# TensorE products whose results nobody reads, in stages that have no work for it

## The chip, the cores and the metric

The kernel runs on one core of one Trainium2 chip. The metric is device time in microseconds (us), lower is better. TensorE is the matrix engine (PE in the profile, its weight loads PEld), VectorE is DVE, ScalarE is ACT, GpSimd is POOL and SyncE (SP) issues the loads. TensorE's clock is granted at one of two levels, 1.2 and 2.4 GHz; the profile writes the granted clock as a share of 2.4 GHz.

## The reference, cut to what matters

Two transformer layers on one sequence of 512 tokens with 1024 features, all in float32. Everything that is computed matters here only as a row of stages: products (TensorE), and between them norms and selections (the other engines).

```python
# layer 1
h = rms_norm(x, ln1_g);  proj = h @ w_in
aq, ak = rms_norm(q, q_norm_g), rms_norm(k, k_norm_g)          # per head of 64
attn = rms_norm(neighbourhood_attention(aq, ak, av, rpb), attn_out_g)
dn   = rms_norm(gated_delta_both_directions(...), out_norm_g) * silu(z)   # q, k l2-normed per head of 128
x = x + concat([attn, dn]) @ w_out
h = rms_norm(x, ln2_g)
#   64 experts in 8 groups: best group, best two experts in it, for each of 512 tokens
y[token] += gate * (silu(h @ w_gate[e]) * (h @ w_up[e])) @ w_down[e]
# layer 2
h = rmsnorm(x);  proj = h @ w_in2
merged = sigmoid(g_ml)*(mlstm(...) @ w_ml) + sigmoid(g_sc)*(short_conv(...) @ w_sc) + sigmoid(g_sb)*(stick_breaking(...) @ w_sb)
x = x + merged @ w_out2
x = x + square(relu(rmsnorm(x) @ w_up2)) @ w_down2
return rmsnorm(x)
```

## The kernel before

The program is a list of 54 stages. Each engine runs its part of stage k, drains its pipeline, adds one to its own counter and waits until the three others (of TensorE, ScalarE, VectorE and GpSimd) have done the same (`close`, L2402 and L2405). So a stage is as long as its longest engine, and an engine that has no part in a stage stands at that barrier. `together()` joins several parts into one stage. SyncE doesn't take part in the barrier and loads weights ahead of it, into four buffers.

Big products (`dense`, `mlp`, `experts`) read 1 MB units of weights, which ScalarE and VectorE split into a high and a low float32r part (`whi`, `wlo`); TensorE makes three products of each pair (high*high, high*low, low*high), 512 columns each, into PSUM banks (L325, L342, L1575, L1589, L2308, L2323). Small things, such as transposes (`transposes`, L396), gram matrices and the delta rule, go in plain float32; of such a product the trace has two records at 128x512, one where it is a transpose.

The stages that the change touches:

- `normalise`: ScalarE squares, VectorE sums and scales. TensorE has no part. It comes nine times before `transposes` of what was normalised (`n1`, `nq`+`nk`, `nao`, `ndq`+`ndk`, `ndo`, `n2`, `h2an`, `ny`+`h2bn`, `h3n`).
- `transposes`: TensorE transposes four 128x128 tiles into each of up to eight banks; ScalarE takes each bank (L406) and, where the result is split, VectorE takes it again (L414).
- `gate_z` and `split_into` (`smix`) around the transposes of the delta rule's result, and then the dense stage `wout`.
- `beta_exp`, a short stage ahead of `delta`. In `delta`, `pe_gram` (L949) makes two products for the first batch; VectorE and ScalarE make `lo_m` and `pw` from them, on which `pe_step` (L967, L969) waits.
- `route` ends on VectorE, `select` builds the one-hot matrices `sel` on VectorE and GpSimd, `sort_tokens` multiplies with them (L1433).
- `combine` gathers the experts' rows by DMA and adds them to `x` on VectorE; it and the norm `h2an` follow each other, then come transposes and a small product (`small_product`, L673).
- `stick`: TensorE makes the scores of heads 0 and 1 (L2152, operands of 64 partitions, and the mask L2157), then `sums(0)` (L2169) waits for ScalarE's and VectorE's softplus of head 0.

Of the kernel before, what the change touches and what calls it, by code (L numbers as in the profile page):

```python
# [33 lines left out]
TT = T // P  # L34
D = 1024
# [48 lines left out]
def build(nc, x_in, cols_in, rows_in, consts_in, bias_in, w_in, w_ab, w_out, w_router, w_gate, w_up, w_down,  # L84
# [186 lines left out]

    def dense(tag, sources, mode, out_fn, by, acc_hi=act_hi, acc_lo=act_lo, loaded=0, lent=None, act_also=None, dve_also=None, pool_part=None):
# [224 lines left out]
    normalise("n1", x[:, :, :], xn[:, :, :], stat_a[:, 0:TT], stat_b[:, 0:TT], D, sq_b[:, :])  # L497
# [19 lines left out]
    with together():  # L517
        normalise("nq", heads64(q_tok), heads64(q_tok), stat_q[:, 0, :], stat_q[:, 1, :], DA, sq_a[:, 0, :], extra=DA ** -0.5)
        normalise("nk", heads64(k_tok), heads64(k_tok), stat_q[:, 2, :], stat_q[:, 3, :], DA, sq_a[:, 1, :])
# [119 lines left out]
    with together():  # L639
        load_small("ab", w_ab, ab_w)  # L640
        normalise("nao", o_tok[:, :, :], attn_n[:, :, :], stat_q[:, 0, 0:TT], stat_q[:, 1, 0:TT], 512, sq_o[:, :])
# [164 lines left out]
    with together():  # L806
        normalise("ndq", heads128(dq_tok), heads128(dq_tok), stat_d[:, 0, :], stat_d[:, 1, :], DD, sq_d[:, :], eps_scale=1.0, extra=DD ** -0.5)
        normalise("ndk", heads128(dk_tok), heads128(dk_tok), stat_d[:, 2, :], stat_d[:, 3, :], DD, sq_e[:, :], eps_scale=1.0)
# [79 lines left out]
    beta_exp()  # L888

    def delta():  # L890
# [109 lines left out]
        def pe_part(pe):  # L1000
            pe_gram(pe, batches[0])
            for a in batches:
                old = batches[a.b - 1] if a.b else None
                new = batches[a.b + 1] if a.b + 1 < NB else None
                for s in range(n_steps):
                    for hb in range(2):
                        pe_step(pe, a, s, hb)
                        if old and s == 0 and hb == 1:
                            pe_scan_out(pe, old, 0)
                        if old and 1 <= s <= 3:  # L1010
                            (pe_scan_out if hb else pe_scan_pv)(pe, old, s)
                    if new and s == 5:
                        pe_gram(pe, new)
            pe_scan_out(pe, batches[-1], 0)
            for n in range(1, TT):
                pe_scan_pv(pe, batches[-1], n)
                pe_scan_out(pe, batches[-1], n)
# [191 lines left out]
    normalise("ndo", heads128(dn_o), heads128(dn_n), stat_d[:, 0, :], stat_d[:, 1, :], DD, dn_sq[:, :])  # L1209
# [11 lines left out]
    gate_z()  # L1221
# [16 lines left out]
    split_into("smix", mix, act_hi, act_lo)  # L1238
# [11 lines left out]
    normalise("n2", x[:, :, :], xn2[:, :, :], stat_m[:, 0, :], stat_m[:, 1, :], D, sq_m[:, :])  # L1250
# [166 lines left out]
    select()  # L1417
# [378 lines left out]
    combine()  # L1796
# [10 lines left out]
    def hidden(tag, gain, also=lambda: None):  # L1807

        with together():
            also()  # L1810
            normalise(tag + "n", x[:, :, :], xn3[:, :, :], stat3[:, 0, :], stat3[:, 1, :], D, sq3[:, :])
        transposes(tag + "t", lambda tt, c: xn3[:, tt, c * P:(c + 1) * P], lambda c: col(gain, c))
# [220 lines left out]
    with together():  # L2033
        normalise("ny", yh, yh, stat_y[:, 0, :], stat_y[:, 1, :], DM, sq_y[:, :])
        normalise("h2bn", x[:, :, :], xn3[:, :, :], stat3[:, 0, :], stat3[:, 1, :], D, sq3[:, :])
# [101 lines left out]
    def stick():  # L2137
# [7 lines left out]
        def pe_part(pe):  # L2145
# [37 lines left out]
            scores(1)  # L2183
            for h in range(HS):
                sums(h)
                if h:
                    values(h - 1)
                if h + 2 < HS:
                    scores(h + 2)
# [325 lines left out]
```

## Time and profile before

| | |
|---|---|
| runs of the kernel before | 2804.57, 2872.67, 2864.63 us; median 2864.63 |
| profiled execution, its own time | 2804.5 us |
| its span, first to last instruction | 2802.7 us |
| mean granted TensorE clock in it | 0.938 |
| TensorE busy / weight loads busy | 88% / 75% |
| VectorE / ScalarE / GpSimd busy | 51% / 41% / 12% |
| chain that ended last: TensorE's share | 81% |

The runs lie 68 us apart, and the profiled execution stands beside the shortest of them. All times of the trace below are of that execution, counted from the span's start.

### The profile page before, as it was taken

The page shows a single profiled execution, that of the slowest core. Times are in us where ns is not written, and L with a number is a line of the kernel's source. Part 1 is how long each engine was busy: PE and PEld are TensorE (multiplying, and loading weights), DVE is VectorE, ACT ScalarE, POOL GpSimd, SP SyncE. Part 2 cuts the span into 40 slices and gives each one's busy share as a digit, 9 for nine tenths or more (in the row PEclk, how much of TensorE's full clock was granted, in tenths as well). Part 3 has the DMA queues.
Part 4 walks back from the last instruction along what each step waited for, and adds up shares of the span by engine and source line. Part 5 has one row for each costly group of instructions (what it writes and reads, how often), then busy time and mean ns, then how long its engine had stood idle before and what let it go on. Part 6 is the DMA issues. An engine that isn't in the chain of part 4 may idle for free.

```text
span 2802.7 us, 34731 instructions
## 1 busy us (share of the span) xinstructions
PE 2458.5 (88%) x13304; PEld 2111.1 (75%) x13304; DVE 1434.1 (51%) x1602; ACT 1139.5 (41%) x1350; POOL 339.2 (12%) x178
## 2 busy tenths in 40 slices
PE   5789789863999999997599659999999998899997
PEld 4567679852899999997488448888887887688885
DVE  2344656636399999997321462253222444434333
ACT  2453455321477777775222232212223651222221
POOL 0000010001245445552100000000000000000000
PEclk9899889985999999999799789999999989899998
DMA  5101000020399999998233002223322001132320
GB/s 211 61 2 61 1 1 1 15 95 16 124 377 378 380 380 379 382 382 306 106 97 98 30 1 90 90 90 106 100 95 90 1 1 60 60 106 92 103 90 38
DMA packets 144427, 356.93 MB, mean 127 GB/s; under 512 B 6496, under 2 KB 82400, under 8 KB 127808
## 3 DMA queue, kind: packets, MB, share of 16 engines
q1 hardware_dynamic: 142736, 346.63, 34.8%
q0 software_dynamic: 1584, 8.78, 0.8%
q8 instruction: 78, 1.28, 0.2%
q14 instruction: 29, 0.24, 0.0%
HBM read 336.52 MB, written 18.87 MB: 127 GB/s over the span
## 4 chain that ended last, share of the span: by engine, by line
PE 81%; DVE 9%; ACT 4%; DMA 2%; issue 2%; DVEq 1%; ACTq 1%; POOL 0%; SPq 0%; POOLq 0%; PEldq 0%
PE PS L325 23%; PE PS L342 11%; PE PS L1589 10%; PE PS L2308 6%; PE PS L2323 6%; PE PS L1575 6%; PE PS L969 4%; PE PS L2169 2%; PE PS L396 2%; PE PS L2152 1%; PE PS L2179 1%; PE PS L1433 1%; DVE wlo L249 1%; PE PS L546 1%; PE PS L563 1%
## 5 line engine op out<-in xcount | busy, mean ns | idle before, releaser
L249 DVE TENSOR_TENSOR wlo<-raw,whi 128x2048 fp32r<-128x2048 f32 x246 | 601.6, 2446 | 654.1 <-ACT whi L242 654.1
L242 ACT ACTIVATE whi<-raw 128x2048 fp32r<-128x2048 f32 x246 | 470.4, 1913 | 535.6 <-PE PS L325 180.0
L325 PE MATMUL PS<-act_hi,whi 128*128 128x512 f32 x736 | 286.6, 389 | 3.1 <-DVEq L2402 3.1
L325 PE MATMUL PS<-act_hi,wlo 128*128 128x512 f32 x736 | 286.4, 389 | 0.0
L325 PE MATMUL PS<-act_lo,whi 128*128 128x512 f32 x736 | 286.3, 389 | 0.0
L1553 POOL TENSOR_TENSOR st_lo<-sorted_h,st_hi 128x512 fp32r<-128x512 f32 x64 | 189.6, 2962 | 11.6 <-POOL st_hi L1550 11.6
L342 PE MATMUL PS<-whi,act_hi 128*128 128x512 f32 x448 | 176.6, 394 | 15.8 <-DVEq L2402 15.8
L342 PE MATMUL PS<-wlo,act_hi 128*128 128x512 f32 x448 | 176.1, 393 | 0.0
L342 PE MATMUL PS<-whi,act_lo 128*128 128x512 f32 x448 | 175.9, 393 | 0.0
L249 DVE TENSOR_TENSOR wlo_x<-raw,whi_x 128x2048 fp32r<-128x2048 f32 x64 | 145.7, 2276 | 36.1 <-ACT whi_x L242 36.1
L325 PEld LDWEIGHTS PS<-act_hi,whi 128*128 128x128 f32 x736 | 138.2, 188 | 32.0 <-issue 3.4
L325 PEld LDWEIGHTS PS<-act_hi,wlo 128*128 128x128 f32 x736 | 138.2, 188 | 28.8
L325 PEld LDWEIGHTS PS<-act_lo,whi 128*128 128x128 f32 x736 | 138.2, 188 | 28.5
L1589 PE MATMUL PS<-whi,st_hi 128*128 128x256 f32 x520 | 153.1, 295 | 7.0 <-POOL st_lo L1553 6.9
L1589 PE MATMUL PS<-wlo,st_hi 128*128 128x256 f32 x520 | 147.8, 284 | 0.0
L1589 PE MATMUL PS<-whi,st_lo 128*128 128x256 f32 x520 | 147.4, 284 | 0.0
L1589 PE MATMUL PS<-whi_x,st_lo 128*128 128x256 f32 x504 | 142.7, 283 | 0.0
L1589 PE MATMUL PS<-wlo_x,st_hi 128*128 128x256 f32 x504 | 142.6, 283 | 0.0
L1589 PE MATMUL PS<-whi_x,st_hi 128*128 128x256 f32 x504 | 142.3, 282 | 0.0
L2382 POOL DMA_DIRECT2D gfin<-in_gfin x1 | 0.5, 546 | 1115.3 <-DVEq L2402 1115.3
L1550 POOL CAST st_hi<-sorted_h 128x512 fp32r x64 | 98.0, 1532 | 263.8 <-PE PS L1589 165.9
L242 ACT ACTIVATE whi_x<-raw 128x2048 fp32r<-128x2048 f32 x64 | 122.2, 1910 | 0.7 <-issue 0.3
(507 smaller groups left out, 5233.2 us busy)
## 6 DMA issues: line engine op xcount, KB each, us to landing
raw<-in_w_up SPq DMA_DIRECT2D x80, 1024.0 KB, 5.4
raw<-in_w_down SPq DMA_DIRECT2D x80, 1024.0 KB, 5.2
raw<-in_w_in SPq DMA_DIRECT2D x66, 1024.0 KB, 5.2
raw<-in_w_gate SPq DMA_DIRECT2D x64, 1024.0 KB, 5.9
y_sorted<-y_sb SPq DMA_DIRECT2D x64, 256.0 KB, 4.7
raw<-in_w_out SPq DMA_DIRECT2D x8, 1024.0 KB, 5.2
raw<-in_w_ml SPq DMA_DIRECT2D x4, 1024.0 KB, 5.2
raw<-in_w_sc SPq DMA_DIRECT2D x4, 1024.0 KB, 5.4
```

Of the source, the lines that this page charges most:

```text
L242: nc.scalar.activation(parts(u, wide)[0], raw[:, raw_slot(u), :], ACT.Copy).then_inc(hi_ready, 1)
L249: nc.vector.tensor_tensor(lo, raw[:, raw_slot(u), :], hi.bitcast(F32), ALU.subtract).then_inc(lo_ready, 1)
L325: last = nc.tensor.matmul(ps[:, m, :], a, b, start=(c == 0 and k == 0), stop=(c == KT - 1 and k == 2))
L342: last = nc.tensor.matmul(psum_of(j, i)[:, m, :], a, b, start=(f == 0 and k == 0), stop=(f == KT - 1 and k == 2))
L396: last = nc.tensor.transpose(PS[:, bank + c % 8, tt * P:(tt + 1) * P], src_tile(tt, c), ident)
L969: last = nc.tensor.matmul(o, lhsT[:, hb, tt, :], rhs[:, hb, tt, :], start=True, stop=True)
L1550: nc.gpsimd.tensor_copy(st_hi[:, b, :, 0:blk], src).then_inc(s_cp, 1)
L1553: nc.gpsimd.tensor_tensor(st_lo[:, b, :, 0:blk], src, st_hi[:, b, :, 0:blk].bitcast(F32), ALU.subtract).then_inc(s_stat, 1)
L1575: i = nc.tensor.matmul(PS[:, 3 + 2 * b + half, :], x_[:, b, j, :], w_[:, j, c], start=(j == 0 and k == 0), stop=(j == 1 and k == 2))
L1589: i = nc.tensor.matmul(PS[:, b, k * DE:(k + 1) * DE], x_[:, b, c, :], w_[:, c, :], start=(c == 0 and m == 0), stop=(c == KT - 1 and m == 2))
L2308: i = nc.tensor.matmul(PS[:, 2 * j + m, :], a_, b_, start=(k == 0 and n == 0), stop=(k == KT - 1 and n == 2))
L2323: i = nc.tensor.matmul(PS[:, 4 * p + m, :], a_, b_, start=(y == 0 and n == 0), stop=(y == KT - 1 and n == 2))
```

## The change

A helper `throwaway(n)` gives TensorE n plain float32 products: stationary `ident` (128x128), moving the first four constant matrices side by side (128x512), into PSUM bank 7, each one with start and stop set. They wait for nothing but the stage's start and signal nothing. Thirteen calls join a stage in which TensorE had no part (`hidden` is called twice, so there are fourteen such stages), and two stand in the middle of TensorE's part: 8 products in bank 5 after the first `pe_gram` of `delta`, and 6 after the scores of heads 0 and 1 in `stick`. The last norm, `nf`, gets none. In all 142 products are added: 5, 12, 6, 12, 2, 8, 6, 5, 6, 6, 13, 26, 6, 17, 6 (stick) and 6 (`h3n`). Nothing else is changed.

```diff
--- before.py
+++ after.py
@@ -269,6 +269,14 @@
         stages.append({e: one_after_another([m[e] for m in members if e in m])
                        for e in ("sp", "pe", "act", "dve", "pool") if any(e in m for m in members)})
 
+    def throwaway(n, bank=7):
+
+
+        def pe_part(pe):
+            for _ in range(n):
+                nc.tensor.matmul(PS[:, bank, :], ident, consts[:, 0:4, :].rearrange("p a b -> p (a b)"), start=True, stop=True)
+        return pe_part
+
     def dense(tag, sources, mode, out_fn, by, acc_hi=act_hi, acc_lo=act_lo, loaded=0, lent=None, act_also=None, dve_also=None, pool_part=None):
 
 
@@ -494,7 +502,9 @@
             split_lo(dve, u, u)
 
     add_stage(sp=first_sp, act=first_act, dve=first_dve, pe=lambda pe: pe.wait_ge(s_load, 7 * 16), pool=first_pool)
-    normalise("n1", x[:, :, :], xn[:, :, :], stat_a[:, 0:TT], stat_b[:, 0:TT], D, sq_b[:, :])
+    with together():
+        add_stage(pe=throwaway(5))
+        normalise("n1", x[:, :, :], xn[:, :, :], stat_a[:, 0:TT], stat_b[:, 0:TT], D, sq_b[:, :])
     transposes("t1", lambda tt, c: xn[:, tt, c * P:(c + 1) * P], lambda c: col("ln1", c))
 
 
@@ -515,6 +525,7 @@
     def heads64(t):
         return t[:, :, :].rearrange("p t (h e) -> p (t h) e", e=DA)
     with together():
+        add_stage(pe=throwaway(12))
         normalise("nq", heads64(q_tok), heads64(q_tok), stat_q[:, 0, :], stat_q[:, 1, :], DA, sq_a[:, 0, :], extra=DA ** -0.5)
         normalise("nk", heads64(k_tok), heads64(k_tok), stat_q[:, 2, :], stat_q[:, 3, :], DA, sq_a[:, 1, :])
     with together():
@@ -638,6 +649,7 @@
         add_stage(pool=lambda pool, st: pool.dma_start(w_f32[:, :, :], w_dram).then_inc(s_small, 16))
     with together():
         load_small("ab", w_ab, ab_w)
+        add_stage(pe=throwaway(6))
         normalise("nao", o_tok[:, :, :], attn_n[:, :, :], stat_q[:, 0, 0:TT], stat_q[:, 1, 0:TT], 512, sq_o[:, :])
     transposes("tao", lambda tt, c: attn_n[:, tt, c * P:(c + 1) * P], lambda c: col("attn_out", c), n_c=4, dst_f32=mix)
 
@@ -804,6 +816,7 @@
     sq_d = at("sq_d", o_w + 8 * KB, [P, TT * 512])
     sq_e = at("sq_e", o_w + 16 * KB, [P, TT * 512])
     with together():
+        add_stage(pe=throwaway(12))
         normalise("ndq", heads128(dq_tok), heads128(dq_tok), stat_d[:, 0, :], stat_d[:, 1, :], DD, sq_d[:, :], eps_scale=1.0, extra=DD ** -0.5)
         normalise("ndk", heads128(dk_tok), heads128(dk_tok), stat_d[:, 2, :], stat_d[:, 3, :], DD, sq_e[:, :], eps_scale=1.0)
     dqT = at("dqT", o_b, [P, HD, T])
@@ -885,7 +898,9 @@
             dve.wait_ge(s_e, 1)
             nc.vector.tensor_tensor(bexp[:, :, :], t_a[:, :, :], beta[:, :, :], ALU.mult)
         add_stage(act=act_part, dve=dve_part)
-    beta_exp()
+    with together():
+        add_stage(pe=throwaway(2))
+        beta_exp()
 
     def delta():
 
@@ -999,6 +1014,7 @@
 
         def pe_part(pe):
             pe_gram(pe, batches[0])
+            throwaway(8, 5)(pe)
             for a in batches:
                 old = batches[a.b - 1] if a.b else None
                 new = batches[a.b + 1] if a.b + 1 < NB else None
@@ -1206,7 +1222,9 @@
     dn_sq = at("dn_sq", o_b, [P, TT * 512])
     dn_z = at("dn_z", o_b + 8 * KB, [P, TT, 512])
     dn_n = at("dn_n", o_b + 16 * KB, [P, TT, 512])
-    normalise("ndo", heads128(dn_o), heads128(dn_n), stat_d[:, 0, :], stat_d[:, 1, :], DD, dn_sq[:, :])
+    with together():
+        add_stage(pe=throwaway(6))
+        normalise("ndo", heads128(dn_o), heads128(dn_n), stat_d[:, 0, :], stat_d[:, 1, :], DD, dn_sq[:, :])
 
     def gate_z():
         s_z = local("gz")
@@ -1218,7 +1236,9 @@
             dve.wait_ge(s_z, 1)
             nc.vector.tensor_tensor(dn_n[:, :, :], dn_n[:, :, :], dn_z[:, :, :], ALU.mult)
         add_stage(act=act_part, dve=dve_part)
-    gate_z()
+    with together():
+        add_stage(pe=throwaway(5))
+        gate_z()
     mix_d = mix[:, 4:8, :]
     transposes("tdn", lambda tt, c: dn_n[:, tt, c * P:(c + 1) * P], lambda c: col("dn_out"), n_c=4, dst_f32=mix_d)
 
@@ -1235,7 +1255,9 @@
                 dve.wait_ge(s_h, c // 2 + 1)
                 nc.vector.tensor_tensor(lo[:, c:c + 2, :], src[:, c:c + 2, :], hi[:, c:c + 2, :].bitcast(F32), ALU.subtract)
         add_stage(act=act_part, dve=dve_part)
-    split_into("smix", mix, act_hi, act_lo)
+    with together():
+        add_stage(pe=throwaway(6))
+        split_into("smix", mix, act_hi, act_lo)
 
     def residual_out(eng, st, j, ps, ms):
         s = slice((j // 2) * 512, (j // 2 + 1) * 512)
@@ -1247,7 +1269,9 @@
     sq_m = at("sq_m", o_b, [P, TT * D])
     o_r = o_w + 36 * KB
     stat_m = at("stat_m", o_r, [P, 2, TT])
-    normalise("n2", x[:, :, :], xn2[:, :, :], stat_m[:, 0, :], stat_m[:, 1, :], D, sq_m[:, :])
+    with together():
+        add_stage(pe=throwaway(6))
+        normalise("n2", x[:, :, :], xn2[:, :, :], stat_m[:, 0, :], stat_m[:, 1, :], D, sq_m[:, :])
     NR = NG + NE
     r_w = at("r_w", o_b, [P, KT, NR])
     r_wh = at("r_wh", o_b + 3 * KB, [P, KT, NR], F32R)
@@ -1414,7 +1438,9 @@
             for tt in range(TT - 1):
                 nc.gpsimd.tensor_scalar(sel_t[:, tt, :], iota[:, :], dest[:, 0, tt:tt + 1], None, ALU.is_equal).then_inc(s_first, 1)
         add_stage(act=act_part, dve=dve_part, pool=pool_part)
-    select()
+    with together():
+        add_stage(pe=throwaway(13))
+        select()
 
     def sort_tokens():
 
@@ -1793,7 +1819,9 @@
                     st.then(nc.vector.scalar_tensor_tensor(x[:, tt, :], y_rows[:, k, tt, :], gates[:, k, tt:tt + 1], x[:, tt, :],
                                                            ALU.mult, ALU.add))
         add_stage(sp=sp_part, pool=pool_part, dve=dve_part)
-    combine()
+    with together():
+        add_stage(pe=throwaway(26))
+        combine()
 
 
 
@@ -1808,6 +1836,7 @@
 
         with together():
             also()
+            add_stage(pe=throwaway(6))
             normalise(tag + "n", x[:, :, :], xn3[:, :, :], stat3[:, 0, :], stat3[:, 1, :], D, sq3[:, :])
         transposes(tag + "t", lambda tt, c: xn3[:, tt, c * P:(c + 1) * P], lambda c: col(gain, c))
 
@@ -2031,6 +2060,7 @@
     sq_y = at("sq_y", o_b, [P, TT * D])
     yh = y_tok[:, :, :].rearrange("p t (h e) -> p (t h) e", e=DM)
     with together():
+        add_stage(pe=throwaway(17))
         normalise("ny", yh, yh, stat_y[:, 0, :], stat_y[:, 1, :], DM, sq_y[:, :])
         normalise("h2bn", x[:, :, :], xn3[:, :, :], stat3[:, 0, :], stat3[:, 1, :], D, sq3[:, :])
     transposes("ty", lambda tt, c: y_tok[:, tt, c * P:(c + 1) * P], lambda c: col("ml", c), dst_hi=y_hi, dst_lo=y_lo)
@@ -2181,6 +2211,7 @@
                 last.then_inc(s_av, 1)
             scores(0)
             scores(1)
+            throwaway(6)(pe)
             for h in range(HS):
                 sums(h)
                 if h:
```

Three places of TensorE's order. Between `route` (products with `both`) and `sort_tokens` (products with `sel`), before:

```order
L1381 MATMUL PS<-both,consts 128x64
L1383 MATMUL PS<-both,consts 128x64 x4
L1433 MATMUL PS<-sel,tok_hi 128x512
L1433 MATMUL PS<-sel,tok_lo 128x512
L1433 MATMUL PS<-sel,tok_hi 128x512
L1433 MATMUL PS<-sel,tok_lo 128x512
```

and with the change:

```order
L1405 MATMUL PS<-both,consts 128x64
L1407 MATMUL PS<-both,consts 128x64 x4
L277 MATMUL PS<-consts 128x512 x13
L1459 MATMUL PS<-sel,tok_hi 128x512
L1459 MATMUL PS<-sel,tok_lo 128x512
L1459 MATMUL PS<-sel,tok_hi 128x512
L1459 MATMUL PS<-sel,tok_lo 128x512
```

The thirteen products stand in the stage `select`, between the two; the products around them are the same, at new line numbers.

At the start of `delta`, after the last products of `grams` (with `g`), TensorE's order before:

```order
L834 MATMUL PS<-g,consts 128x4
L835 MATMUL PS<-g,consts 128x4
L949 MATMUL PS<-qeT_129,consts 128x512 x2
L967 MATMUL PS<-consts,pw_119 128x128 x8
L969 MATMUL PS<-pw_119,pwT 128x128 x4
L969 MATMUL PS<-pwT,pw_119 128x128 x4
```

and with the change:

```order
L847 MATMUL PS<-g,consts 128x4
L848 MATMUL PS<-g,consts 128x4
L277 MATMUL PS<-consts 128x512 x2
L964 MATMUL PS<-qeT_129,consts 128x512 x2
L277 MATMUL PS<-consts 128x512 x8
L982 MATMUL PS<-consts,pw_119 128x128 x8
L984 MATMUL PS<-pw_119,pwT 128x128 x4
L984 MATMUL PS<-pwT,pw_119 128x128 x4
```

Two products stand ahead of the gram products (with `qeT`), in the stage `beta_exp`, and eight between those and the transposes of `pw`.

At the start of `stick`, the scores of head 1 (`bqT`, `bkT`, mask) and then the sums of head 0 (`sb_hi`, `sb_lo`), on TensorE before:

```order
L2152 MATMUL PS<-bqT,bkT 128x384
L2152 MATMUL PS<-bqT,bkT 128x256
L2152 MATMUL PS<-bqT,bkT 128x128
L2157 MATMUL PS<-sb_mask,sb_id 128x128 x4
L2169 MATMUL PS<-sb_hi_237,sb_tri 128x512
L2169 MATMUL PS<-sb_lo_234,sb_tri 128x512
L2169 MATMUL PS<-sb_hi_237,sb_one 128x384
```

and with the change:

```order
L2182 MATMUL PS<-bqT,bkT 128x384
L2182 MATMUL PS<-bqT,bkT 128x256
L2182 MATMUL PS<-bqT,bkT 128x128
L2187 MATMUL PS<-sb_mask,sb_id 128x128 x4
L277 MATMUL PS<-consts 128x512 x6
L2199 MATMUL PS<-sb_hi_237,sb_tri 128x512
L2199 MATMUL PS<-sb_lo_234,sb_tri 128x512
L2199 MATMUL PS<-sb_hi_237,sb_one 128x384
```

Six products stand between head 1's mask and head 0's sums.

## Rows read from the trace of the kernel before

**Rows 1.** The page's first two parts: TensorE's busy time, granted clock in slices.

```profile
PE 2458.5 (88%) x13304; PEld 2111.1 (75%) x13304; DVE 1434.1 (51%) x1602; ACT 1139.5 (41%) x1350; POOL 339.2 (12%) x178
...
PEclk9899889985999999999799789999999989899998
```

**Rows 2.** Windows of stages without TensorE: length, busy PE, PEld, DVE, ACT, POOL, PEclk.

```profile
108.10:120.40 12.30, 0.00 (x0) 0.00 (x0) 10.67 (x15) 4.72 (x10) 0.00 (x0) 0.50 0.26 85
203.60:210.00 6.40, 0.00 (x0) 0.00 (x0) 5.11 (x7) 3.68 (x6) 0.55 (x1) 0.74 0.04 10
...
352.00:353.90 1.90, 0.00 (x0) 0.00 (x0) 0.19 (x1) 1.51 (x2) 0.00 (x0) 0.88 0.00 0
...
572.70:578.70 6.00, 0.00 (x0) 0.00 (x0) 4.63 (x4) 3.90 (x4) 0.00 (x0) 0.72 0.00 0
628.50:635.30 6.80, 0.00 (x0) 0.00 (x0) 5.47 (x10) 3.68 (x6) 0.00 (x0) 0.50 0.44 154
684.60:698.30 13.70, 0.00 (x0) 0.00 (x0) 12.28 (x9) 3.90 (x4) 10.34 (x3) 0.50 0.00 0
1326.80:1353.10 26.30, 0.00 (x0) 0.00 (x0) 10.28 (x8) 0.00 (x0) 7.65 (x8) 0.50 0.78 280
...
1641.80:1658.70 16.90, 0.00 (x0) 0.00 (x0) 14.83 (x17) 7.68 (x11) 0.00 (x0) 0.56 0.00 0
...
sum 134.90, PE 0.00 PEld 0.00 DVE 97.78 ACT 52.90 POOL 19.13; mean PE 0.00 PEld 0.00 DVE 6.98 ACT 3.78 POOL 1.37
```

**Rows 3.** Timeline of TensorE in delta, batches 0 and 1: start, length.

```profile
355.43 3.75 PE L949 MATMUL PS<-qeT,consts 128*128 128x512 f32 x4 [3.71 <-ACT qeT L1048]
363.95 0.47 PE L967 MATMUL PS<-consts,pw 128*128 128x128 f32 x1 [4.77 <-DVE lo_m L1131]
...
387.62 1.88 PE L949 MATMUL PS<-qeT,consts 128*128 128x512 f32 x4
389.34 0.83 PE L969 MATMUL PS<-pw,pwT 128*128 128x128 f32 x6
```

**Rows 4.** Windows where TensorE had work, same columns as Rows 2.

```profile
336.20:339.80 3.60, 3.47 (x17) 3.50 (x18) 0.00 (x0) 1.79 (x3) 0.00 (x0) 0.50 0.00 0
353.40:370.50 17.10, 10.03 (x31) 6.61 (x32) 9.93 (x30) 10.05 (x32) 7.18 (x4) 0.50 0.00 0
578.70:582.10 3.40, 3.35 (x8) 2.70 (x9) 0.00 (x0) 0.00 (x0) 0.00 (x0) 0.50 0.00 0
698.30:701.60 3.30, 3.25 (x8) 2.68 (x9) 0.00 (x0) 0.00 (x0) 0.52 (x1) 0.50 0.00 0
1363.80:1367.20 3.40, 1.71 (x16) 1.47 (x14) 3.30 (x6) 2.86 (x5) 0.00 (x0) 1.00 0.00 0
2159.10:2176.20 17.10, 16.03 (x42) 11.07 (x43) 6.83 (x10) 9.76 (x17) 0.00 (x0) 0.50 0.20 62
```

**Rows 5.** Timeline of TensorE around two transposing stages; idle before in brackets.

```profile
27.37 6.23 PE L396 MATMUL PS<-consts,xn 128*128 128x128 f32 x32 [27.37 <-DVEq L2402]
35.68 0.48 PE L342 MATMUL PS<-whi,act_hi 128*128 128x512 f32 x1 [2.08 <-DVEq L2402]
...
36.39 0.63 PE L342 MATMUL PS<-whi,act_lo 128*128 128x512 f32 x1
...
1359.98 5.54 PE L396 MATMUL PS<-consts,xn 128*128 128x128 f32 x32 [35.80 <-DVEq L2402]
1368.64 0.40 PE L673 MATMUL PS<-act_hi,g2h 128*8 128x512 f32 x1 [3.13 <-DVE g2l L663]
```

**Rows 6.** Groups by line: VectorE's and ScalarE's reading of transposed banks.

```profile
L414 DVE SCALAR_TENSOR_TENSOR act_lo<-PS,cols,act_hi 128x512 fp32r<-128x512 f32 x40 | 28.3, 747 | 11.9 <-ACT act_hi L406 10.4
...
L406 ACT ACTIVATE act_hi<-PS,cols 128x512 fp32r<-128x512 f32 x40 | 25.9, 687 | 22.0 <-PE PS L396 21.5
```

**Rows 7.** Timeline of TensorE at the start of stick.

```profile
2169.25 1.11 PE L2157 MATMUL PS<-sb_mask,sb_id 128*128 128x128 f32 x4
...
2172.38 0.69 PE L2169 MATMUL PS<-sb_hi,sb_one 128*128 128x384 f32 x1 [1.06 <-DVE sb_lo L2244]
```

## The prediction

> **What bounds the kernel now.** The page comes first: TensorE is busy for 88% of the span, no other engine for over 51% [rows 1]. So the end is set by TensorE's work and by the stages that keep it waiting at the barrier. The line PEclk shows that the granted clock is well below full in 11 of the forty slices [rows 1]. Windows over single stages say why: where TensorE has no work (PE busy 0.00) PEclk is 0.50, which is 1.2 GHz, throughout, or becomes so on the way (0.74 in the stage from 203.6, 0.56 in that from 1641.8) [rows 2]. The work behind such a stage then starts at 1.2 GHz: windows cut to the stretches that were granted 0.50 hold TensorE work in each case [rows 4]. A transposed tile costs 3.47/17 = 0.20 us there and 1.71/16 = 0.107 us at 2.4 GHz. Sooner or later the clock rises: after 3.3 us of sorting products, 3.4 us of dense ones, 3.6 us of transposes (each of these windows ends at the rise). That is what the change works on. It can't touch the large dense stages, which run at full clock already. The mean clock of 0.938 means (1 - 0.938) x 2 x 2802.7 = 347 us at half clock, but most of them hold no TensorE work; in the five windows of [rows 4] that stand at 0.50 there are 3.47 + 10.03 + 3.35 + 3.25 + 16.03 = 36 us of it, of which at most half, 18 us, could go.
>
> **What one added product costs.** Two float32 products of 128x512 are four records: 3.75 us at half clock, 1.88 us at full, and the next operation started 389.34 - 387.62 = 1.72 us behind the first [rows 3]. So a product is 0.86 us at full clock and 1.71 at half; 142 of them are 122 us at full clock. They are free as long as they end before their stage does. The gap of each place is a row:
> - Stages entered with TensorE warm: 6 products, 5.2 us, in 6.4 (203.6; `ndo` is like it) and 6.0 us (572.7); 17, 14.6 us, in 16.9; 2, 1.7 us, in 1.9; 5 and 12 likewise fit [rows 2]. Cost 0; I take 0.2 for `beta_exp`, where the pipeline's drain adds to 1.7.
> - Stages entered after a longer idle, at half clock: until the rise products run at half speed. With 3.4 us to the rise the delay is 1.7 us: 12 products take 10.3 + 1.7 = 12.0 in 12.3 us, 13 take 12.9 in 13.7, 26 take 24.1 in 26.3, but 6 take 6.9 in 6.8 us (628.5, and the norm of each hidden stage) [rows 2]. With 5 us to the rise it would be 0.8 us more in each. I take 1.3 us for the five tight ones. Sum of overruns: 1.5 us lost; bounds 0.2 and 5.
>
> **What is gained behind these stages.**
> - Transposes with a split result, five stages. At half clock TensorE sets the pace: 8 banks x 4 x 0.20 = 6.5 us, then 0.69 and 0.75 for the last bank's readers, 8.0 us (35.68 - 27.37 = 8.3 with the barrier) [rows 4, 5]. At full clock VectorE does: 0.43 + 0.69 + 8 x 0.747 = 7.1 us [rows 6]. So 0.9 us each, not half of TensorE's time: 4.5 us.
> - Transposes into float32, read by ScalarE alone: with four banks 16 x 0.20 + 0.69 = 4.0 against 0.43 + 4 x 0.687 = 3.2 us, twice 0.8; with eight banks twice some 0.5 us, since the clock rises half way now. 2.6 us.
> - `wout` and `sort_tokens` start at full clock: half of 3.35 and of 3.25 us [rows 4], 3.3 us.
> - `delta`: the gram products end at 355.43 + 1.88 = 357.3 instead of 359.2, then eight products fill 6.9 us, until 364.2. The transposes of `pw` began at 363.95 [rows 3], so they begin 0.2 us later than now, although their operand is there some 1.9 us sooner: this block is as long as the wait that it fills. Behind it 10.03 - 3.75 = 6.3 us of work leave half clock [rows 4], 3.1 us, of which I leave 0.5 to evictions. Net 2.4 us gained. If the two products in `beta_exp` don't hold the clock, the block ends at 367.8 and 1.2 us are lost.
>
> **What is given back.** This is the part that the plan of filling idle stages leaves out. Nothing fills the end of a transposing stage. There TensorE now works 6.23 us and idles 2.08 us, and with the third product the clock is at half again (0.63 us for a record at 36.39) [rows 5]. With fast transposes it is done in 3.4 us and idles 3.7 us in a stage of 7.1. The second pair of [rows 5] shows the other side: after 3.13 us idle the clock was still full (0.40 us for the record at 1368.64). I take it that 3.7 us and more lose it nearly always. The price is half of 3.4 us, 1.7, for the product of the gates behind `h2at`, which starts at full clock now; half of that each for attention and for the small product behind `tao`; and 0.3 for each of four places that lose it already. 1.7 + 1.7 + 1.2 = 4.6 us lost; bounds 0 and 9.
>
> **`stick`.** Head 1's mask ends at 2169.25 + 1.11 = 2170.4; head 0's sums wait inside until 2172.38 [rows 7]. Ten us of scores have gone by at half clock, TensorE busy 16.03 of 17.1 us at 0.50 [rows 4], so these products, on 64 partitions, haven't lifted it, and the six new ones start at half: two of them in 3.4 us, four at 0.86, until 2177.3. The sums, 4.3 us at half clock from 2172.4, take 2.3 at full: they end at 2179.6 instead of 2176.7. 3 us later, 1 us of it returned in head 1. 2.0 us lost; bounds 8.5 lost (half clock throughout: 10.3 us) and 1 gained.
>
> **Sum.** 4.5 + 2.6 + 3.3 + 2.4 - 4.6 - 1.5 - 2.0 = 4.7 us gained, 0.2%. The profiled execution's own time is 2804.5 us (span 2802.7 and 1.8 around it), so it would become 2799.8. The runs shown lie 68 us apart, from 2804.57 to 2872.67, and the profiled one is at their short end; their median is 2864.63. Nothing in the trace of one execution explains the 60 us, and the change doesn't aim at them: I carry the difference over to the median, 2864.6 - 4.7 = 2859.9.
>
> **A rule weighed.** Transposes lift the clock here: 17 of them from 336.2 on, rise at 339.8, and 1.00 in the window from 1363.8 on [rows 4]. The Trainium skill, "TensorE: Matmul & The Clock Gate", Part 4: PE-mode transpose, says that the full clock isn't engaged in transpose mode. By that rule the terms of the transposes, 7.1 gained and 4.6 given back, would vanish and the sum would be 2.2 us instead of 4.7; the trace speaks against it.
>
> **Rivals.**
> - The clock holds through the idle ends of the transposing stages. For it: 3.13 us idle kept it once [rows 5]. Then nothing is given back: 9 us gained, up to 14 with `stick` free. 2853.
> - The late rise: the clock comes up a few us later than taken in the stages entered cold and in `stick`, and the blocks overrun. The tight places lose 0.8 us each, `delta` 3.6, `stick` up to 6.5: some 10 us slower than before, 2875. For it: two of the blocks (`delta`, `stick`) stand on the path with no slack.
> - Slower, by one mechanism: the added products themselves don't lift or hold the clock (`ident` and the constants are nearly all zeros; no row shows such a product). Then all 142 take 1.71 us, 243 us, against 134.9 us of stages without work [rows 2], 4.8 in `delta` and 2 in `stick`: 101 us slower, 2966, or 3.6%. It decides from about half of the products at half clock, 56 us. Against it: float32 work on all 128 partitions (transposes, and the steps of `delta` up to 370.5) is followed by a rise in [rows 4].
> - The change does nothing for the clock and costs nothing, because readers (VectorE, ScalarE) set these stages anyway: 2864.6. It is the floor of the first case more than a case of its own.
>
> **How the numbers follow.** Forecast with its terms inside their bounds, or no effect: 0.67. Clock holds: 0.13. Late rise: 0.15. Products at half clock: 0.05. All but the last lie within 2%, about what a measurement of this kernel can tell from no change. One thing lies beside the mechanism: the median of the changed kernel may fall at the short level where the shown median is at the long one; that alone would read 2.3% faster (2800 to 2864.6). I give the place of the median 0.3 and a verdict built on it a fifth of that, 0.06. Faster 0.06, same 0.89, slower 0.05. The range goes from the short level with most gains, 2788, to the longest run with the late rise's loss, 2880; the likeliest case at like level is 2850 to 2866.
>
> **What would show it.** In the profile of the changed kernel: PEclk 1.00 in the stages of [rows 2] but for their first 3 to 5 us; records of the first transposes at 0.107 apart; transposing stages of 7.1 instead of 8.3 us; half clock at the start of what follows them (records of 0.63), the gates' product behind `h2at` above all; `stick`'s sums starting some 7 us behind head 1's mask. Wrong would be: records of the new line that start 0.85 us apart throughout, or stages longer by over 1 us.

## The result, and the profile after

The changed kernel took 2845.99 us (median of six runs, 2826.71 to 2860.36), the kernel before 2834.60 (six runs, 2803.27 to 2872.67). The ratio is 1.0142, 95% interval [1.0076, 1.0208]: 1.4% slower. This ratio, and those below, leave out executions more than 1.5% above the shortest of their kernel, here the three of before near 2868; what those are is part of the answer below. By the medians of all six executions each, the changed kernel is 0.4% slower. The profiled execution took 2860.36 us, 56 more than the one before.

The first two parts of the page after, the same lines as [rows 1]:

```profile
PE 2630.6 (92%) x13588; PEld 2182.0 (76%) x13588; DVE 1427.0 (50%) x1602; ACT 1137.6 (40%) x1350; POOL 338.9 (12%) x178
...
PEclk9857999998899999999899799999999899999998
```

Mean granted clock 0.942 against 0.938. TensorE is busy for 172 us more. PEclk is worse than before in the third and fourth slices (5 and 7, where [rows 1] have 9 and 9), which is 143 to 286 us, and no other loss is as large. The engines' barrier counters, which both traces hold, give the length of each of the 54 stages: a stage lasts from the last engine's step at one barrier to the last engine's step at the next. These are all that differ by over 0.3 us (differences of the unrounded lengths, in us; in brackets the products added in the stage):

```
stage                          before   after    difference
n1 transposes                     8.3     7.1    -1.2
nq, nk (12 products)             12.3    13.6    +1.3
tq, tk transposes                 7.1     5.9    -1.2
attention                        76.2   133.8   +57.6
tao transposes                    4.5     3.3    -1.2
to_tokens                         8.3     8.7    +0.4
tdq, tdk transposes               6.3     4.9    -1.4
beta_exp (2)                      1.9     3.8    +1.8
delta (8)                       202.1   199.4    -2.7
tdn transposes                    4.5     3.3    -1.2
wout                             49.8    48.2    -1.6
n2 (6)                            6.8     7.2    +0.4
t2 transposes                     8.1     7.2    -1.0
sort_tokens                      33.8    32.6    -1.2
experts                         592.9   598.8    +5.9
extra_blocks                      1.9     1.5    -0.4
combine (26)                     26.2    26.8    +0.6
h2at transposes                   7.9     7.1    -0.9
small product g2                  8.0     9.6    +1.6
ty / h2bt transposes         8.3, 7.7  7.1, 8.4  -0.5
branches                        484.3   485.9    +1.6
stick (6)                       150.5   148.7    -1.8
tby transposes                    7.3     6.5    -0.9
wout2                            49.7    50.8    +1.1
h3n (6)                           6.8     8.4    +1.6
h3t transposes                    8.1     7.2    -0.9
```

One stage holds it all. Without attention the sum is 1.7 us in the change's favour. The 5.9 us of `experts`, whose part of the program is the same, are in part scatter: in the ten other traces of this case that stage takes 592.2 to 596.6 us. Why it is longest in this trace was not looked into. The windows after, over attention and what stands before it (columns as in [rows 2]; the second and third lines divide the first):

```profile
106.80:120.50 13.70, 13.52 (x24) 5.56 (x24) 10.68 (x15) 4.72 (x10) 0.00 (x0) 0.78 0.24 77
106.80:112.90 6.10, 5.98 (x7) 2.52 (x8) 4.84 (x8) 4.50 (x9) 0.00 (x0) 0.50 0.54 172
112.90:120.50 7.60, 7.54 (x18) 3.04 (x16) 5.84 (x8) 0.23 (x1) 0.00 (x0) 1.00 0.00 0
120.50:126.40 5.90, 3.69 (x33) 3.48 (x33) 0.00 (x0) 4.73 (x8) 0.00 (x0) 1.00 0.02 4
126.40:249.50 123.10, 123.10 (x373) 83.64 (x374) 28.62 (x102) 39.16 (x89) 0.00 (x0) 0.50 0.00 1
249.50:260.10 10.60, 10.02 (x77) 8.57 (x76) 2.69 (x10) 3.68 (x8) 0.00 (x0) 1.00 0.00 0
```

In the norm's stage the twelve products run, at 0.50 for 6.1 us and then at 1.00. The transposes behind it run at 1.00, TensorE busy for 3.69 of 5.90 us. Attention then stands at 0.50 for 123.1 us with TensorE busy all the time, and its last 10.6 us at 1.00. The timeline of TensorE at that point, after:

```profile
120.83 1.94 PE L404 MATMUL PS<-consts,q_tok 128*128 128x128 f32 x16 [0.39 <-POOLq L2433]
122.60 1.91 PE L404 MATMUL PS<-consts,k_tok 128*128 128x128 f32 x16
126.40 7.05 PE L557 MATMUL PS<-kT,qT 64*128 64x512 f32 x8 [1.88 <-ACTq L2433]
```

TensorE has been idle for 1.88 us when the scores start, and eight score records take 7.05 us. The same place before, with 1.24 us idle and 3.70 us for eight records:

```profile
127.46 3.70 PE L546 MATMUL PS<-kT,qT 64*128 64x512 f32 x8 [1.24 <-ACTq L2402]
```

So attention has two courses. On the short one it lasts 76 us, at full clock. On the long one it stands at half clock, here for 123 us, though TensorE never rests. The groups of attention's products by line, before and then after, show that all three kinds grew:

```profile
L546 PE MATMUL PS<-kT,qT 64*128 64x512 f32 x64 | 31.4, 613 | 1.2 <-ACTq L2402 1.2
L563 PE MATMUL PS<-v_tok,probT 128*128 128x64 f32 x256 | 30.2, 272 | 0.0
L554 PE MATMUL PS<-consts,prob 128*128 128x128 f32 x128 | 17.6, 279 | 0.8 <-ACT prob L592 0.8
```

```profile
L557 PE MATMUL PS<-kT,qT 64*128 64x512 f32 x64 | 58.2, 1062 | 1.9 <-ACTq L2433 1.9
L574 PE MATMUL PS<-v_tok,probT 128*128 128x64 f32 x256 | 50.5, 383 | 0.0
L565 PE MATMUL PS<-consts,prob 128*128 128x128 f32 x128 | 29.7, 408 | 0.0
```

### The profile page after: what moved, and what is told of

Same layout as the page of the kernel before. It is cut to its first block, busy times and chain, and to the rows that moved or that the text cites. A ratio compares the mean times of both kernels' runs of the same rounds, so it can differ in the third digit from the quotient of the medians.

```text
span 2858.6 us, 35299 instructions
## 1 busy us (share of the span) xinstructions
PE 2630.6 (92%) x13588; PEld 2182.0 (76%) x13588; DVE 1427.0 (50%) x1602; ACT 1137.6 (40%) x1350; POOL 338.9 (12%) x178
## 4 chain that ended last, share of the span: by engine, by line
PE 78%; DVE 9%; DMA 4%; ACT 3%; issue 2%; DVEq 1%; ACTq 1%; PEldq 1%; POOL 0%; POOLq 0%; SPq 0%; PEld 0%
PE PS L333 22%; PE PS L350 11%; PE PS L1615 9%; PE PS L2339 6%; PE PS L2354 6%; PE PS L1601 4%; PE PS L984 4%; PE PS L557 2%; DMA raw<-in_w_down 2%; PE PS L574 2%; PE PS L2199 2%; DVE wlo L249 2%; PE PS L2182 2%; PE PS L2209 1%; ACT whi L242 1%
## 5 line engine op out<-in xcount | busy, mean ns | idle before, releaser
L249 DVE TENSOR_TENSOR wlo<-raw,whi 128x2048 fp32r<-128x2048 f32 x246 | 595.0, 2420 | 666.0 <-ACT whi L242 665.7
L277 PE MATMUL PS<-consts 128*128 128x512 f32 x284 | 141.0, 655 | 59.7 <-DVEq L2433 54.9
L277 PEld LDWEIGHTS PS<-consts 128*128 128x128 f32 x284 | 58.3, 210 | 134.3 <-issue 128.3
```

Of the source, the lines that this page charges most:

```text
L249: nc.vector.tensor_tensor(lo, raw[:, raw_slot(u), :], hi.bitcast(F32), ALU.subtract).then_inc(lo_ready, 1)
L277: nc.tensor.matmul(PS[:, bank, :], ident, consts[:, 0:4, :].rearrange("p a b -> p (a b)"), start=True, stop=True)
```

## The experiments

Ten runs, of nine kernels. Each had executions of the kernel before beside it, on the same chip. "Long" is said here of an execution over 2820 us.

**a1_no_nq.** The change without the twelve products ahead of attention's transposes.

```diff
     with together():
-        add_stage(pe=throwaway(12))
         normalise("nq", ...)
```

> The change without the 12 products in the norm ahead of the attention's transposes; all other 130 stay. Entry theory (attention keeps the clock it is entered with, and the 12 products make the transposes ahead of it so fast that TensorE idles 2.3 us at their stage's end and attention is entered at half clock): the transposes take 7.1 us again, attention 76 us at full clock as in the execution before, and the profiled one is at 2858.6 - 57.6 = 2801 us or a little less; runs near 2800, with longer ones by some 60 as the kernel before has them. Shift theory (attention falls to half clock in some executions of any kernel, by the moment at which it is reached; the added products only shift that moment, all alike): the same spread as the changed kernel, 2827 to 2860 in nearly every run. Overrun theory (the loss is a sum of overrunning blocks all over the program): 2 us less than the changed kernel, 2844.

Measured: median 2803.98 us of twelve runs, ratio 0.9985 [0.9951, 1.0018]; profiled span 2800.0, attention 76.2 us, transposes 7.4. Seven runs lie between 2799 and 2806, five at 2827 to 2862. Without twelve of the 142 products the traced execution has the 57 us back and seven of twelve are short, where the changed kernel had none of six; that is what the entry theory had, and the overrun theory is out. Five long runs of twelve are about as many as before has (10 of 28 beside it), so those products aren't the only way into the long course.

**b1_nq_only.** The kernel before with those twelve products and nothing else of the change.

```diff
+    def throwaway(n, bank=7): ...
     with together():
+        add_stage(pe=throwaway(12))
         normalise("nq", ...)
```

> The kernel before with only the 12 products in the norm ahead of the attention's transposes. Entry theory: transposes 5.9 us, attention entered at half clock and 100 to 134 us long, runs 2825 to 2862 in nearly all executions. Shift theory: a mix of 2804 and 2865 as in the kernel before. Overrun theory: 2805, slower by 1.3 us.

Measured: median 2874.26 us of six; 2828.47, four at 2872 to 2876, and one of 6466.22, the profiled one, which tells nothing (one execution of the kernel before beside it took 5125.56). There was no short run. That speaks for entry, but without a trace that can be read:

**b2_nq_only_again.** The same kernel.

> The kernel before with only the 12 products ahead of the attention's transposes, the same kernel as the second run, whose profiled execution took 6466 us and can't be read. Entry theory: a profile in which attention is entered at half clock and is 100 to 136 us long, the runs 2828 to 2876. Shift theory: about one execution in four near 2865, the rest 2803.

Measured: median 2857.43 us; 2817.41, 2837.56, 2857.16, 2857.70, 2858.19 and 2868.70 us, ratio 1.0125 [1.0061, 1.0189]; seven of eleven executions of before beside it were under 2810. The 2817.41 lies below the 2828 that the entry theory had named. In the trace attention lasts 127.2 us. Windows of the transposes, attention's start and what follows, and then TensorE's timeline across that start:

```profile
118.00:123.00 5.00, 4.55 (x35) 3.51 (x33) 0.69 (x1) 3.15 (x6) 0.00 (x0) 1.00 0.02 5
124.80:127.20 2.40, 2.40 (x6) 1.09 (x7) 1.20 (x4) 0.25 (x1) 0.00 (x0) 1.00 0.01 3
127.20:236.50 109.30, 109.30 (x340) 75.40 (x339) 25.23 (x92) 36.10 (x83) 0.00 (x0) 0.50 0.00 1
...
124.67 4.68 PE L555 MATMUL PS<-kT,qT 64*128 64x512 f32 x8 [1.89 <-ACTq L2411]
```

Twelve products alone reproduce the whole loss (1.0125 against 1.0142). The clock is full through the transposes and through the first 2.4 us of this stretch, then half for 109.3 us. Here attention was entered at full clock and lost it right away, behind its first scores, so "entered at half clock" is a little too narrow. What the traces have in common is what TensorE did before the clock fell: in the three of the long course (the changed kernel, this one and `d1_burst`) it was idle for 1.88 or 1.89 us ahead of attention's scores; in traces of the short course it was idle for 1.24 us (before), 1.00 (`a1_no_nq`), 0.33 (`h1_bridge_only`) and 0.23 (`c1_bridge`). No run moves this idle time alone.

**c1_bridge.** The change, and two more products behind the transposes ahead of attention.

```diff
         transposes("tk", ..., n_c=4, dst_f32=kT, bank=4)
+
+        def bridge(pe):
+            pe.wait_ge(s_tq, 1)
+            throwaway(2, 0)(pe)
+        add_stage(pe=bridge)
```

> The change, and 2 more products (bank 0, once ScalarE has taken it) behind the transposes ahead of attention, so that TensorE isn't idle at that stage's end. Entry theory: attention is entered at full clock and takes 76 us; the whole is 2858.6 - 57.6 = 2801 us, in nearly all runs, so narrower than before and after. Shift theory: no difference to the changed kernel. If 2 products are too few or attention's first us are themselves too thin, some runs stay long: 2825 to 2860.

Measured: median 2799.58 us of twelve runs, all between 2795.60 and 2805.82; ratio 0.9971 [0.9947, 0.9994]. Of before's 28 ordinary executions beside it ten were over 2820. The timeline of TensorE in this kernel:

```profile
120.67 1.94 PE L404 MATMUL PS<-consts,q_tok 128*128 128x128 f32 x16 [0.23 <-POOLq L2439]
122.45 1.91 PE L404 MATMUL PS<-consts,k_tok 128*128 128x128 f32 x16
124.19 1.88 PE L277 MATMUL PS<-consts 128*128 128x512 f32 x4
126.31 3.67 PE L563 MATMUL PS<-kT,qT 64*128 64x512 f32 x8 [0.23 <-ACTq L2439]
```

and windows over the transposes' stage and attention:

```profile
120.50:126.20 5.70, 5.40 (x36) 4.12 (x36) 0.00 (x0) 4.73 (x8) 0.00 (x0) 1.00 0.00 1
126.30:202.40 76.10, 74.72 (x448) 53.64 (x448) 30.73 (x112) 42.63 (x97) 0.00 (x0) 1.00 0.00 1
```

The transposes are as fast as in the changed kernel, and TensorE works 5.40 of 5.70 us of their stage, against 3.69 of 5.90. Attention lasts 76.1 us at 1.00. Two products of 0.86 us return the 57.6. They both take the idle time away and add two products of another kind; the runs don't part these two.

**h1_bridge_only.** The kernel before with those two products, and none of the change's 142.

```diff
+    def throwaway(n, bank=7): ...
         transposes("tk", ...)
+        def bridge(pe): ...            # the same
+        add_stage(pe=bridge)
```

> The kernel before with none of the 142 products, and only 2 products behind the transposes ahead of attention. Entry theory: the long executions of the kernel before (10 of 28 over 2820 us) are attention entered at half clock too, so none of the runs of this kernel is over 2815; the others at 2803 + 0.7 us, since the bridge ends 0.5 us behind ScalarE. Shift theory, or another cause of the long executions: a quarter to a third of the runs over 2820 as before.

Measured: 2803.10 to 2816.20 us in six runs, none long, beside four long ones of eleven of before (2839.10 to 2863.43). Median 2807.23, ratio 0.9991 [0.9951, 1.0030]. One of the six, 2816.20, is above the 2815 that the entry theory had named. So the 60 us that separate the two kinds of executions of the kernel before are, by all that these runs show, attention on its long course too. No trace of a long execution of before was taken; six runs without one would come about once in fifteen times if four in eleven were still long, and with the 12 of c1_bridge and the 12 of the two filled kernels below, none long either, it is no longer chance.

The mean granted clock, which the profiler gives for every execution, points the same way. With each span it gives the time at half clock, (1 - clock) x 2 x span, to some 3 us. In the short executions of before, beside any of these runs, that is 342 to 359 us; in its 16 long ones from 2857 to 2868 it is 457 to 482, some 120 us more. Attention stands at half clock for 123.1 us in the changed kernel's trace and costs 57.6 us there: the same amount of half-clock time at the same price. The six executions of h1_bridge_only have 347 to 355 us. The twelve of c1_bridge have 201 to 213, and the six of the changed kernel 260 to 332, each at least 47 us more, and more where the execution is longer.

**d1_burst.** The change, and eight products inside attention, ahead of the transposes of unit 8 of 32.

```diff
             def turn(u):
                 ...
+                if u == 8:
+                    throwaway(8, 4 + u % 2)(pe)
                 for kt in range(TT):
```

> The change, and 8 products inside attention ahead of the transposes of unit 8 of 32. Entry theory, in the form that attention keeps either clock: half clock up to the burst, then full: 8 of 32 units at 4.1 us each, the burst 10 us, the rest at 2.4 us: about 33 + 10 + 57 = 100 us, the whole 2825. If attention's own work can't hold the full clock when it is entered cold, the clock falls again behind the burst: 134 + 10, the whole 2868.

Measured: median 2824.21 us, twelve runs of 2810.53 to 2833.12, ratio 1.0049 [1.0023, 1.0074]; attention 100.0 us in the trace, where 100 was expected. Windows of attention up to the rise and behind it:

```profile
127.40:164.90 37.50, 37.50 (x103) 23.16 (x102) 9.73 (x36) 14.66 (x33) 0.00 (x0) 0.50 0.00 1
164.90:225.00 60.10, 59.49 (x358) 43.03 (x356) 20.23 (x73) 28.14 (x64) 0.00 (x0) 1.00 0.00 1
```

Half clock up to the burst, at 162.3, full 2.6 us into it, and full from there for at least 60 us. Here attention's own products hold the full clock once they have it, and don't bring it back soon when they haven't. That is why a 2 us cause has a 60 us price. The runs of the changed kernel are spread over 34 us because, as their clocks say, the long course ends at some moment of its own, at 249.5 in the trace of the changed kernel. Two of the twelve runs, 2810.53 and 2813.85 us, have 208 us at half clock, no more than c1_bridge: up to the burst this is the changed kernel, so that kernel too misses the long course at times.

**f1_fill_all.** The bridged change, with the idle end of the other transposing stages filled as well.

```diff
     def transposes(..., bank=0, fill=0):
         def pe_part(pe):
             ...
+            if fill:
+                pe.wait_ge(s_h, 1)
+                if dst_f32 is None:
+                    pe.wait_ge(s_d, 1)
+                throwaway(fill, bank)(pe)
...
# fill=3 for t1, t2, h2at, ty, h2bt, tby, h3t; fill=1 for tao, tdn; beta_exp: throwaway(1)
```

> The bridged change, and the idle end of the other transposing stages filled too: 3 products behind each of the split ones, 1 behind the two with four banks; 1 instead of 2 in the stage ahead of delta. If what is given back behind the transposes is the clock lost in their idle end: the small products take 8.3 us instead of 9.3 to 9.8, branches 484.3 instead of 485.9, wout2 and the first MLP unit 1 us less each: some 6 us below the bridged change, 2791. If it isn't: the same 2797, or more where a fill ends behind its stage's readers.

Measured: median 2793.36 us, 2784.16 to 2796.90; ratio 0.9936 [0.9897, 0.9975]. It beats both kernels, the one before by 0.6% in its short executions. The small product for `g2` takes 8.0 us (9.3 in c1_bridge), the one for `ab` 8.3 (9.8), the router's 9.3 (11.5), `branches` 484.3 (485.9), the MLP 349.8 (351.4): 8.2 us in these. Not all of it is the fill's: `ab` and `g2` take 8.3 and 8.0 us in the kernel before as well, and in kernels that are the same as it from attention on they take 9.8 and 9.5 (b2_nq_only_again) or 8.3 and 9.3 (h1_bridge_only). The `branches` and the MLP are clearer: 484.3 and 349.8 in all three filled kernels, 485.9 and 351.4 in all five with the other fillers only. `wout2` did not get its 1 us: 51.0 (50.8).

The profiled execution itself, span 2795.1, shows only a part, since `stick` took 155.3 us in it (148.7 in c1_bridge). That is the clock again. Windows of `stick` at half clock, in the filled kernel and in c1_bridge:

```profile
2170.80:2191.30 20.50, 20.50 (x75) 17.71 (x74) 4.93 (x8) 9.22 (x14) 0.00 (x0) 0.50 0.00 1
...
2177.00:2183.80 6.80, 6.80 (x29) 6.38 (x27) 1.87 (x4) 3.80 (x6) 0.00 (x0) 0.50 0.00 0
```

Both begin 24 us into the stage; one lasts 20.5 us and the other 6.8, TensorE busy throughout, and half of that difference, 6.9 us, is about the 6.5 by which the stage is longer. After the change, `g2` had begun at full clock and fallen to half five records later, behind 4.12 us idle (timeline of TensorE):

```profile
1414.84 3.69 PE L404 MATMUL PS<-consts,xn 128*128 128x128 f32 x32 [1.41 <-DVEq L2433]
1422.64 0.40 PE L685 MATMUL PS<-act_hi,g2h 128*8 128x512 f32 x1 [4.12 <-DVE g2l L675]
...
1423.56 0.55 PE L685 MATMUL PS<-act_hi,g2l 128*8 128x512 f32 x1
1423.91 0.63 PE L685 MATMUL PS<-act_lo,g2h 128*8 128x512 f32 x1
```

and in the filled kernel it stays at 0.40 us a record behind three products and 1.56 us idle:

```profile
1349.56 3.68 PE L404 MATMUL PS<-consts,xn 128*128 128x128 f32 x32 [1.42 <-DVEq L2444]
1353.08 2.74 PE L277 MATMUL PS<-consts 128*128 128x512 f32 x6
1357.37 0.39 PE L696 MATMUL PS<-act_hi,g2h 128*8 128x512 f32 x1 [1.56 <-DVE g2l L686]
...
1358.53 0.40 PE L696 MATMUL PS<-act_lo,g2h 128*8 128x512 f32 x1
```

**g1_no_stick** and **k2_fill_no_stick.** The bridged and the filled version without the six products in `stick`.

```diff
             scores(1)
-            throwaway(6)(pe)
             for h in range(HS):
```

> The bridged change without the six products in stick. The prediction's step (they start at half clock, end 5 us too late and cost 2 us): stick some 2 to 3 us shorter than its 148.7, 146. The other reading (they lift the clock ahead of the first sums, and head 0's chain on ScalarE and VectorE sets the pace anyway): 150.5 us, as in the kernel before.

> The filled version without the six products in stick. In the filled version's profile stick took 155.3 us, in the changed kernel's 148.7, both with the six products; without them, in the bridged version, 150.3. If the six products decide nothing and stick's length goes by where its thin work lets the clock fall: 148 to 156 us again, and runs of 2784 to 2797 as the filled version. If they are worth 1.6 us each time: the runs 1 to 2 us longer, 2795.

Measured: `stick` 150.3 us in the first (one run, 2801.56), 152.2 in the second (median 2795.17 of six, 2790.33 to 2796.90; ratio 0.9954 [0.9938, 0.9970]). Over all traces: with the six products 148.7 (the changed kernel, c1_bridge, d1_burst), 150.7 (k1_no_delta), 150.8 (a1_no_nq) and 155.3 (f1_fill_all); without them 148.3 (b2_nq_only_again), 150.3, 150.4 (h1_bridge_only), 150.5 (before) and 152.2. Their effect is smaller than the stage's own scatter, and the runs around the medians, 2793.36 and 2795.17, overlap. Neither the prediction's 2 us lost nor a gain of 1.6 is shown.

**k1_no_delta.** The filled version without the product ahead of `delta` and without the eight in it.

```diff
-    with together():
-        add_stage(pe=throwaway(1))
-        beta_exp()
+    beta_exp()
...
             pe_gram(pe, batches[0])
-            throwaway(8, 5)(pe)
```

> The filled version without the product ahead of delta and without the 8 behind its first gram products. The prediction's step (the 8 fill the wait and 2.4 us of half-clock work behind it go): the two stages take 204.0 us as in the kernel before, 0.7 us less in the changed kernel's 203.2. If what counts is only whether the clock is up at 363, the difference to the filled version (1.9 + 202.8 = 204.7 us) is under 1 us either way.

Measured: 1.9 + 201.2 = 203.1 us for the two stages; 203.2 in the changed kernel, 204.0 before, 204.7 in the filled one (one run, 2790.78). The expectation had 204.0. The nine products' effect isn't separated from scatter here: k2_fill_no_stick, which has them, takes 1.9 + 200.9 = 202.8 us. Over all traces the two stages take 204.0 or 204.1 us in the three kernels without any of the change there (before, b2_nq_only_again, h1_bridge_only), and 202.0 (a1_no_nq) and four times 203.2 or 203.3 in the five with all of it: 0.8 us or more in favour of the ten products and the warm stages ahead together. The timeline of TensorE at this place in the changed kernel:

```profile
407.33 2.72 PE L277 MATMUL PS<-consts 128*128 128x512 f32 x3
411.53 2.20 PE L964 MATMUL PS<-qeT,consts 128*128 128x512 f32 x4 [1.48 <-ACT qeT L1064]
413.57 7.03 PE L277 MATMUL PS<-consts 128*128 128x512 f32 x16
420.44 1.04 PE L982 MATMUL PS<-consts,pw 128*128 128x128 f32 x8
```

The eight fill 7.03 us as forecast, and what follows runs at full clock; but the two in `beta_exp` started at half clock and took the stage to 3.8 us.

## Why the prediction was wrong

It gave 0.2% faster, and it was 1.4% slower by the ratio above. That the median of 2845.99 us lies inside the range of 2788 to 2880 is luck: the range was wide because before had two levels, and nothing in it stood for what happened. By its steps:

- **The failed step** is in "What is given back": "half of that each for attention and for the small product behind `tao`", 0.9 us for attention. The place and the direction were right (fast transposes leave TensorE idle at their stage's end, and the clock falls at the start of what follows); the size was taken from dense products, which bring the clock back in 3.4 us. Attention's don't. It measured 57.6 us in the profiled execution, over sixty times the term. The prediction had the hint beside it: it argued for `stick` that ten us of scores on 64 partitions hadn't lifted the clock, and attention begins with the same kind of product. It never asked how long attention would take to come back.
- The second miss is "Nothing in the trace of one execution explains the 60 us, and the change doesn't aim at them". True of the trace, but by what h1_bridge_only, c1_bridge and the clocks show the 60 us between runs are this same stage, and the change does touch them: the long course, which before takes in a third to two thirds of its executions (10 of 28, 4 of 11, 8 of 12 over 2820 us), became one that all six have.
- One added product: 0.86 us at full clock, right (16 records in 7.03 us).
- Transposes: 5.3 us for the five with a split result (forecast 4.5), 5.0 for the others (2.6). Those with four banks take 3.3 us, near the 3.2 of the forecast, but had taken 4.5 where it had 4.0; those with eight gained 1.2 and 1.4 us each, not 0.5.
- `wout` and `sort_tokens`: 2.8 us (3.3). `delta`: 2.7 (2.4), but `beta_exp` cost 1.8 where 0.2 was taken, since its two products started at half clock.
- Overruns, apart from `beta_exp`: 4.0 us (1.3) in `nq`, `n2`, `combine`, `h3n`. In `nq` the rise came 6.1 us into the stage and not at the 3.4 taken, as the late-rise rival had it. `combine` took 25.0 to 27.0 us over all kernels, so its 0.6 can be scatter.
- Given back outside attention: g2 1.6 (forecast 1.7). That agrees in part by luck: b2_nq_only_again and h1_bridge_only, which are the kernel before from attention on, lose 1.5 and 1.3 us there too. The product behind `tao` (0.9) lost nothing, 8.3 us before and after. h2bt, branches and wout2 cost 3.5 together; of these only the 1.6 of the branches comes back in every kernel with fast transposes and without the fill.
- `stick`: forecast 2.0 lost, measured 1.8 gained, and not separable from scatter. Its six products did start at half clock, and ended 16.8 us into the stage where 18.3 was forecast.
- The slower rival, that the products don't hold the clock, is out: in the norm's stage, where TensorE has nothing else, PEclk went from 0.50 to 1.00 after 6.1 us of them and stayed there. The time came out on the slower side by another mechanism than the one listed.

What stays open: why attention takes the long course in one execution of a kernel and not in another, why it leaves it at one moment and not another, whether the idle time ahead of it is the cause or the kind of work that fills it, and why `experts` varies by some 6 us between kernels.

## What to carry to other kernels

Before filling an engine's idle time to keep its clock, ask of every stage behind it whether its own work can bring the clock back; where it can't, the clock at its entry is worth the whole stage, and the filler belongs directly ahead of it, not a stage earlier. Work that gets faster ends earlier, and its new idle end can be the one that matters. When runs of one kernel fall into two groups, find the stage that has two lengths before predicting anything: here two small products in the right place took the long executions away, and 142 spread over the program without them made all six of them long.

## What the runs showed of the hardware

- One and the same stage, with the same products, ran 76 us at a granted clock of 1.00 (c1_bridge, TensorE busy 74.72 of 76.10 us) or stood at 0.50 for 123.10 us with TensorE busy in all of them (the changed kernel). Its mix: scores on 64 partitions, transposes, and products of 64 columns.
- A burst of eight float32 products of 128x512 inside it was followed by the full clock 2.6 us after its start, and the clock held for the 60.10 us looked at (d1_burst).
- The Trainium skill, "TensorE: Matmul & The Clock Gate", Part 4: PE-mode transpose, says that the full clock isn't engaged in transpose mode. In the windows after, the transposing stage from 120.5 stands at 1.00 throughout (behind the twelve products), and before, with no work of TensorE ahead of them, 17 transposes were followed by the rise [rows 4]: the trace doesn't agree.
